# A transformer block on one core: the input projection on the unnormalised x, with w_ada's product moved to the output stage

## What is computed

```python
def rms_norm(x, g):
    y = x * rsqrt(mean(x * x, -1) + 1e-6) * g

h = rms_norm(x, norm_mix_pre)
proj = h @ w_in                      # 1024 x 2560: q, k, v and 14 tiles for the time mix
p = p + (p_prev - p) * rwkv_shift_mix          # p_prev: p moved by one token
scores = q @ k.T * scale + rel_bias[bucket(rel)]   # attention's bias table
...
x = x + rms_norm(mix @ w_out, norm_mix_post)   # the output stage
...
shift, scale, gate = split(silu(c) @ w_ada + b_ada, 3)   # used first behind the FFN
```

## Time and profile before

| what | us |
|---|---|
| runs: median of 3 (lowest, highest) | 3296.24 (3292.69, 3300.53) |
| profiled execution: span, first to last instruction | 3291.8 |
| TensorE matmul busy | 2815.3 (86%) |
| VectorE busy | 1213.9 (37%) |
| ScalarE busy | 726.0 (22%) |
| GpSimd busy | 795.9 (24%) |

### The profile page before, as it was taken

How to read it: one execution, slowest core, us unless ns; L and a number is a source line. 1 busy time by engine, 2 the same in 40 slices (tenths; PEclk the granted TensorE clock), 3 DMA queues, 4 the chain that set the end, 5 groups by cost and what they waited for, 6 DMA issues and landing times.

```text
span 3291.8 us, 45652 instructions
## 1 busy us (share of the span) xinstructions
PE 2815.3 (86%) x17970; PEld 2240.3 (68%) x17970; DVE 1213.9 (37%) x1572; ACT 726.0 (22%) x1050; POOL 795.9 (24%) x448
## 2 busy tenths in 40 slices
PE   2999766888889779999999999994999947879886
PEld 1787446878776558888888888882788836653375
DVE  2544554344443363213313313316100055544343
ACT  2101551111121222102102202102101253225521
POOL 1344000000001223433434343340333333210011
PEclk7999676687789889999999999996899955558988
DMA  5411000000001011111111111112111100000031
GB/s 162 154 39 57 0 18 15 2 3 3 2 28 71 32 71 51 51 45 51 45 51 45 51 49 47 51 45 115 75 59 51 39 26 1 0 3 1 0 122 58
DMA packets 34892, 146.85 MB, mean 45 GB/s; under 512 B 3656, under 2 KB 5832, under 8 KB 33608
## 3 DMA queue, kind: packets, MB, share of 16 engines
q1 hardware_dynamic: 23184, 84.42, 7.6%
q10 hardware_dynamic: 11576, 60.50, 5.0%
HBM read 124.46 MB, written 20.45 MB: 44 GB/s over the span
## 4 chain that ended last, share of the span: by engine, by line
PE 76%; DVE 14%; ACT 5%; issue 3%; DMA 2%; DVEq 1%; ACTq 0%; POOL 0%; POOLq 0%
PE ps L370 52%; PE ps L715 2%; PE ps L531 2%; ACT ab L76 1%; DVE s_m L76 1%; PE ps L768 1%; DVE x_lo L76 1%; DVE proj L76 1%; DVE xx L76 1%; PE ps L556 1%; DVE ps L76 1%; DMA bias_table<-bias_row 1%; PE ps L547 1%; PE ps L530 1%; DVE zz L76 1%
## 5 line engine op out<-in xcount | busy, mean ns | idle before, releaser
L302 POOL TENSOR_TENSOR w_hi<-w_raw,small 128x1024 fp32r<-128x1024 f32 x161 | 306.2, 1902 | 2256.6 <-PE ps L370 2249.8
L370 PE MATMUL ps<-x_hi,w_hi 128*128 128x512 f32 x2064 | 647.4, 395 | 85.1 <-DVE x_lo L76 78.7
L370 PE MATMUL ps<-x_lo,w_hi 128*128 128x512 f32 x2064 | 643.1, 393 | 0.0
L370 PE MATMUL ps<-x_hi,w_lo 128*128 128x512 f32 x2064 | 641.7, 392 | 0.0
L370 PEld LDWEIGHTS ps<-x_hi,w_hi 128*128 128x128 f32 x2064 | 388.7, 190 | 179.7 <-issue 72.4
L370 PEld LDWEIGHTS ps<-x_lo,w_hi 128*128 128x128 f32 x2064 | 392.4, 190 | 82.8
L370 PEld LDWEIGHTS ps<-x_hi,w_lo 128*128 128x128 f32 x2064 | 391.9, 190 | 82.7
L305 POOL TENSOR_TENSOR w_lo<-w_raw,w_hi 128x1024 fp32r<-128x1024 f32 x161 | 406.0, 2522 | 12.7
L76 DVE SCALAR_TENSOR_TENSOR cv<-ps,cst,cv 128x1023 f32<-128x1023 f32 x64 | 82.1, 1282 | 258.1 <-ACT cv L76 252.7
L370 PE MATMUL ps<-f_hi,w_lo 128*128 128x512 f32 x512 | 157.6, 389 | 0.0
L370 PE MATMUL ps<-f_hi,w_hi 128*128 128x512 f32 x512 | 157.6, 389 | 0.0
(11 more groups left out here) (255 smaller groups left out, 3917.4 us busy)
## 6 DMA issues: line engine op xcount, KB each, us to landing
w_raw<-wall SPq DMA_DIRECT2D x161, 512.0 KB, 3.4
ada_w<-wada ACTq DMA_DIRECT2D x24, 512.0 KB, 5.4
x_spill<-x ACTq DMA_DIRECT2D x2, 4096.0 KB, 11.0
x<-x_spill ACTq DMA_DIRECT2D x2, 4096.0 KB, 13.3
x_in<-xT ACTq DMA_DIRECT2D x2, 2048.0 KB, 12.0
x<-xT ACTq DMA_DIRECT2D x1, 4096.0 KB, 13.6
gate_spill<-gate_st ACTq DMA_DIRECT2D x8, 512.0 KB, 2.6
gate_in<-gate_spill ACTq DMA_DIRECT2D x8, 512.0 KB, 3.4
```

The costliest lines, as they stand in the source:

```text
L302: nc.gpsimd.tensor_tensor(w_hi[:, u, :, :], w_raw[:, u, :, :], sm["one"].unsqueeze(2).to_broadcast([P, KT, P]), ALU.mult).then_inc(S("w_hi ...
L370: last = mm(ps[:, 2 * u + h, :], w[:, u, k, :], x[:, k, h * 512:(h + 1) * 512], start=(k == 0 and w is w_hi and x is hi), stop=(k == KT - ...
```

## The change

The parameters that are needed first stand at the front of `cst` and are loaded by themselves; the rest follows behind x, which comes in eight loads of one tile. ScalarE makes x_hi straight from `x * g` as a tile lands, and its square after it; VectorE makes x_lo. TensorE takes gemm 0 one column at a time as x_lo comes, gemm 1 two columns behind it, with a norm sum after the even steps 2 to 8 of both; gemm 2 goes into banks 6 and 7. VectorE takes the reciprocal into `rs0` and evicts all twenty gemms itself, times `rs0` (`scaled`). The bias product comes behind gemm 3, its table is written and read while ScalarE has only one copy to make. w_ada's loads (a ring of four, three ahead of each y1 tile), the 24 steps of `modulation` (six ahead of each pair sum) and its products move to the output stage. Events that happen once share three semaphores (`once`); the lines that differ by that alone are left out below, as are the ones for `pairs_of`, `ada_w` and `ada_acc`, which get other places in SBUF.

```diff
@@ tensor
-            pe.wait_ge(S("cst_in"), 16)
-            pe.wait_ge(S("neg_row"), 1)
-            mm(ps[0:8, 0, 0:384], par("rel_bias", ...), par("onehot", ...))...(S("bias_mm"), 1)
-            norm_sum(0)
-            pe.wait_ge(S("bias_cp"), 1)
-            gemm(0, 0, x_hi, x_lo, first=True, parts=("x_lo_done", 0))
-            gemm(1, 1, x_hi, x_lo, first=True)
-            gemm(2, 0, x_hi, x_lo)
+            pe.wait_ge(S("par_in"), 16)
+            pe.wait_ge(S("w_split"), 1)
+            for step in range(KT + 2):
+                if step < KT:
+                    pe.wait_ge(S("x_lo_done"), step + 1)
+                    last = column(0, 0, step)
+                    if step == KT - 1:
+                        last.then_inc(S("gemm_mm"), 1)
+                if step == 2:
+                    pe.wait_ge(S("w_split"), 2)
+                if step >= 2:
+                    last = column(2, 1, step - 2)
+                    if step == KT + 1:
+                        last.then_inc(S("gemm_mm"), 1)
+                if step in (2, 4, 6, 8):
+                    norm_part(0, step // 2 - 1)
+            pe.wait_ge(S("w_split"), 3)
+            for k in range(KT):
+                last = column(6, 0, k)
+            last.then_inc(S("gemm_mm"), 1)
             gemm(3, 1, x_hi, x_lo)
+            pe.wait_ge(S("cst_in"), 16)
+            pe.wait_ge(*once("neg_row"))
+            pe.wait_ge(*once("rs0_done"))
+            mm(ps[0:8, 4, 0:384], par("rel_bias", ...), par("onehot", ...))...(once("bias_mm")[0], 1)
             gemm(4, 0, x_hi, x_lo)
             gemm(5, 1, x_hi, x_lo)
-            pe.wait_ge(S("one"), 1)
-            pe.wait_ge(S("ada_acc"), ADA_N)
-            for j in range(ADA_N):
-                last = mm(ps[:, 7, j:j + 1], ada_acc[...], sm["one"], start=True, stop=True)
-            last.then_inc(S("ada_mm"), 1)
+            gemm(6, 0, x_hi, x_lo)
             pe.wait_ge(S("gemm_evac"), 6)
-            turn(raw[:, 1, :], 4)
-            with pe.Fori(3, 10) as i:
+            turn(raw[:, 1, :], 6)
+            gemm(7, 1, x_hi, x_lo)
+            with pe.Fori(4, 10) as i:
...
             norm_sum(1)
+            pe.wait_ge(S("gemm_evac"), G_FFN)
+            pe.wait_ge(S("ada_acc"), ADA_N)
+            for j in range(ADA_N):
+                last = mm(ps[:, 0, j:j + 1], ada_acc[...], sm["one"], start=True, stop=True)
+            last.then_inc(once("ada_mm")[0], 1)
             norm_sum(2)
+            pe.wait_ge(*once("ada_done"))
@@ scalar
-            act.dma_start(x_in[:, 0:4, :], ...).then_inc(S("x_in0"), 16)
-            act.dma_start(x_in[:, 4:8, :], ...).then_inc(S("x_in1"), 16)
-            act.dma_start(cst[:, :], dr["cst"]).then_inc(S("cst_in"), 16)
+            act.dma_start(cst[:, 0:N_PAR], dr["cst"][:, 0:N_PAR]).then_inc(S("par_in"), 16)
+            for k in range(KT):
+                act.dma_start(x_in[:, k, :], dr["xT"][:, k * T:(k + 1) * T]).then_inc(S(f"x_in{k}"), 16)
+            act.dma_start(cst[:, N_PAR:], dr["cst"][:, N_PAR:]).then_inc(S("cst_in"), 16)
...
+            act.wait_ge(S("par_in"), 16)
+            for k in range(KT):
+                act.wait_ge(S(f"x_in{k}"), 16)
+                fn(x_hi[:, k, :], x_in[:, k, :], ACT.Identity, scale=par("g_mix_pre", k, 1))...
+                if k >= 2:
+                    act.wait_ge(S("norm_pair"), k // 2)
+                fn(sq_a[:, k % 2, :], x_in[:, k, :], ACT.Square).then_inc(S("norm_sq"), 1)
+            root(0)
+            act.wait_ge(*once("bias_mm"))
             copy(bias_row[0:8, :], ps[0:8, 4, 0:384])...
             act.dma_start(bias_dram, bias_row...).then_inc(S("bias_out"), 16)
+            act.wait_ge(S("turn_mm"), 1)
+            copy(proj[:, 5, :], pair(6)).then_inc(S("turn_cp"), 1)
             act.wait_ge(S("bias_out"), 16)
             act.dma_start(bias[:, :, :], ...).then_inc(S("bias_in"), 16)
-            high(0, lambda k: nrm_a[:, k % 2, :], "h_done")
-            for n in range(ADA_RING, 2 * ADA_RING):
-                ada_load(n)
-            for g in range(6):
-                for n in range(2 * ADA_RING + 3 * g, min(2 * ADA_RING + 3 * g + 3, ADA_N)):
-                    ada_load(n)
-                act.wait_ge(S("gemm_mm"), g + 1)
-                copy(proj[:, g, :] if g < 5 else raw[:, 1, :], pair(2 * (g % 2))).then_inc(S("gemm_evac"), 1)
...
+            act.wait_ge(S("cst_in"), 16)
+            fn(sm["silu_c"], par("c"), ACT.Silu).then_inc(once("c_silu")[0], 1)
             def y1_tile(k):
                 g = G_OUT + k
+                for n in range(3 * k, 3 * k + 3):
+                    ada_load(n)
                 act.wait_ge(S("gemm_mm"), g + 1)
                 copy(y1[:, k, :], pair(2 * (g % 2))).then_inc(S("gemm_evac"), 1)
@@ vector
-            for j in range(4):
-                norm_pair(0, j)
-            apply_all(0, 0, nrm_a, ...)
-            for n in range(ADA_N):
-                modulation(n)
-            dve.wait_ge(S("ada_mm"), 1)
-            tt(sm["ada"], ps[:, 7, 0:24], par("b_ada"), ALU.add)
-            ts(sm["ada"][:, 8:16], sm["ada"][:, 8:16], 1.0, None, ALU.add).then_inc(S("ada_done"), 1)
+            for k in range(KT):
+                dve.wait_ge(S("x_hi_done"), k + 1)
+                stt(x_lo[:, k, :], x_in[:, k, :], par("g_mix_pre", k, 1), x_hi[:, k, :].bitcast(F32),
+                    ALU.mult, ALU.subtract).then_inc(S("x_lo_done"), 1)
+                if k % 2:
+                    norm_pair(0, k // 2)
+            dve.wait_ge(S("norm_root"), 1)
+            reciprocal(rs0[:, :], rs_of(0)).then_inc(once("rs0_done")[0], 1)
+            def scaled(g, out, b):
+                dve.wait_ge(S("gemm_mm"), g + 1)
+                tt(out, pair(b), rs0[:, :], ALU.mult).then_inc(S("gemm_evac"), 1)
+            for g in range(5):
+                scaled(g, proj[:, g, :], 6 if g == 2 else 2 * (g % 2))
+            scaled(5, raw[:, 1, :], 2)
             def shift(g, j, s):
-                dve.wait_ge(S("gemm_evac"), g + 1)
+                scaled(g, raw[:, s, :], 2 * s)
                 tt(dif[:, s, 1:], raw[:, s, 0:T - 1], raw[:, s, 1:], ALU.subtract)
...
+            dve.wait_ge(*once("c_silu"))
             for j in range(4):
+                for n in range(6 * j, 6 * j + 6):
+                    modulation(n)
                 norm_pair(1, j)
...
             norm_pair(2, 3)
+            dve.wait_ge(*once("ada_mm"))
+            tt(sm["ada"], ps[:, 0, 0:24], par("b_ada"), ALU.add)
+            ts(sm["ada"][:, 8:16], sm["ada"][:, 8:16], 1.0, None, ALU.add).then_inc(once("ada_done")[0], 1)
             apply_all(2, 2, nrm_a, ...)
```

More of the change, by code:

```diff
@@ L95, in S, with once @@
             return sems[name]
+        def once(event):
+            sem = next(n for n, events in ONCE.items() if event in events)
+            return S(sem), ONCE[sem].index(event) + 1
         def at(name, shape, unit, dt=F32, off=0):
@@ L380, in turn, with norm_part @@
                 last.then_inc(S("turn_mm"), 1)
+            def norm_part(n, j):
+                pe.wait_ge(S("norm_pair"), 4 * n + j + 1)
+                for h in range(2):
+                    last = mm(rs_of(n)[:, h * 512:(h + 1) * 512], par("mean_all").to_broadcast([P, P]),
+                              pairs_of[n][:, j % 2, h * 512:(h + 1) * 512], start=(j == 0), stop=(j == 3),
+                              skip_group_check=True)
+                last.then_inc(S("norm_mm"), 1)
             def norm_sum(n):
@@ L384, in norm_sum, with column @@
                 for j in range(KT // 2):
-                    pe.wait_ge(S("norm_pair"), 4 * n + j + 1)
+                    norm_part(n, j)
+            def column(b, u, k):
+                for w, x in ((w_hi, x_hi), (w_hi, x_lo), (w_lo, x_hi)):
                     for h in range(2):
-                        last = mm(rs_of(n)[:, h * 512:(h + 1) * 512], par("mean_all").to_broadcast([P, P]),
-                                  pairs_of[n][:, j % 2, h * 512:(h + 1) * 512], start=(j == 0), stop=(j == 3),
+                        last = mm(ps[:, b + h, :], w[:, u, k, :], x[:, k, h * 512:(h + 1) * 512],
+                                  start=(k == 0 and w is w_hi and x is x_hi), stop=(k == KT - 1 and w is w_lo),
@@ L403, in _ @@
-            gemm(2, 0, x_hi, x_lo)
-            gemm(3, 1, x_hi, x_lo)
+                return last
+            pe.wait_ge(S("par_in"), 16)
[14 more added lines that the diff above has]
+                    norm_part(0, step // 2 - 1)
@@ L405, in _ @@
+            pe.wait_ge(S("w_split"), 3)
+            for k in range(KT):
+                last = column(6, 0, k)
+            last.then_inc(S("gemm_mm"), 1)
+            gemm(3, 1, x_hi, x_lo)
+            pe.wait_ge(S("cst_in"), 16)
+            pe.wait_ge(*once("neg_row"))
+            pe.wait_ge(*once("rs0_done"))
+            mm(ps[0:8, 4, 0:384], par("rel_bias", p1=N_BUCKETS + 1), par("onehot", p1=N_BUCKETS + 1),
+               start=True, stop=True).then_inc(once("bias_mm")[0], 1)
             gemm(4, 0, x_hi, x_lo)
```

(6 more changed lines are left out.)

90 lines of the change are left out of this document (40 added, 50 removed).

## The result

The changed kernel takes **3248.62 us** (median of 4 runs, 3247.14 to 3250.62), the kernel before 3294.47 us beside it (4 runs, 3289.98 to 3300.53): ratio 0.9865, interval 0.9851 to 0.9879. That is 45.9 us less, where the prediction had 62.4 less (3233.8) and a range that ended at 3247. The sign was right; the size was wrong, and the median lies 1.6 us outside the range.

A forecast was written before the change was run, and what follows sets the result against it. TensorE's chain bounds the first stage, so an earlier start shortens the end. First stage -70.1, evictions +0.2, output stage +7.5 give -62.4 us: span 3291.8 to 3229.4, median 3233.8, range 3220 to 3247.

The forecast's parts named there:

- the removed wait in attention: Attention: the wait that the change removes was already met long before, so its removal gives 0.
- the shared semaphores: Whole kernel: letting events that happen once share semaphores costs nothing.
- (c): Rival: bias table's write and weight loads hinder each other, three loads up to 5 us late, +15, 3249; chance 0.04.
- (b): Rival, output stage: loads behind x's 4 MB delay ScalarE's evictions, up to 30 us more, 3264; chance 0.07.
- The first stage: From the start to gemm 19's end: ends at 246.2 against 316.3, 70.1 us sooner.
- Start: First GEMM matmul: TensorE starts at 11.5 us, after split 0 and x_lo 0; bounds 10.2 to 12.8.
- Step 2: First stage: waits for split 1 and x_lo 2 until 19.6; TensorE idles 3.1 us, plus 1.1 of clock.
- Norm sums: First stage, steps 2 to 9: four sums of 2.0 us on TensorE's path, 8.0 more.
- Gemm 3: First stage: banks scaled out at 56.8, wanted at 58.7, margin 1.9 us; if missed, 0 to 3 late.
- Bias product and transposes: First stage on TensorE: bias product 0.8 us (between 0 and 2.0), transposes 1.8.
- Evictions: VectorE's evictions are covered under GEMMs; only after gemm 19 open, 1.22 for ScalarE's 1.03: +0.2 us.
- The output stage: Its end: late loads and modulations delay the last pair sum, +7.5 us (bounds +4 and +9); earlier all is slack.

The follow-up runs named there:

- a_mod8: Changed kernel with w_ada's loads four a tile over six output tiles and its products ahead of the first three pair sums: 3239.91 us.
- a_pad64: Changed kernel with 64 empty instructions at the head of TensorE's program: 3225.66 us, ratio 0.9799 to the kernel before.

## Why the prediction was wrong, point by point

**The step that failed** is one that the sum did not have. It went from gemm 19 to the output stage with two zeros ("the removed wait in attention was met long before: 0", "the shared semaphores cost nothing"), taking it that code which the change does not touch runs as before. It does not: the change puts 95 more instructions ahead of TensorE's recurrence loop, and the loop takes 24.0 us more, about 3.4 for each of seven jumps back; 95 empty instructions in the kernel before cost it 23.2 by themselves. The trace of the kernel before held the warning, TensorE's seven gaps of up to 3.9 us on "issue" in that loop, 26 us in all; the prediction reads no view of that stage. No rival named it either; (c) named 3249, nearly the measured time, and (b) up to 3264, but by ways that did not happen: that (c) comes so close is chance. The Trainium skill ("Runtime: NRT & Kernel Launch", section "Instruction fetch mechanics") says that code is fetched in blocks of 256 instructions ahead of use, and that a taken branch whose target is not at hand waits for its block; the gaps at each jump back agree, 3.7 us in the mean before and 4.9 after. With blocks of that size the runs can be put in the order of the head's place (an estimate from that figure: instructions past its place in the kernel before, whole blocks left out): 0, 31 and 63 took 457.9, 458.5 and 459.9 us, 95 took 481.9 and 481.1, 127 took 466.7, 159 took 462.2 and 458.6, 223 took 459.8. So the slow places begin between 63 and 95, and the cost has faded again by 159. That the wait depends on where the head lies the Trainium skill does not say; the runs do. Bounds for that term, an estimate from the rows of the kernel before, would have been, below, nothing, and above, another gap like those there at each jump: 26 us. With them the range would have held the result.

**The first stage** was right, 3.9 us too small: -74.0 for -70.1.
- *Start*: 12.3 for 11.5, within its bounds; but what ended last was x's first tile (7.7) with table load, x_hi and x_lo behind it, not split 0.
- *Step 2*: 18.18 for 19.6, after 1.04 us of idle in place of 3.1, and no 1.1 us of clock behind it: the granted clock is 1.00 from 16 to 44 us. The splits came sooner than in the earlier trace rows, likely since w_ada's loads no longer share the DMA engines with the weight tiles (not tested alone). The mechanism that made x_lo long was right (1.91 and 2.86 us beside splits).
- *Norm sums*: 1.72 us for 2.0. With the earlier step 2, gemm 1 ends at 44.6 for 47.8.
- *Gemm 3*: its banks were scaled out at 53.6, 1.9 us before it wanted them; no wait. That this is the very margin forecast is partly luck, since both times came 3.2 us earlier than forecast. Scaled evictions took 1.23 us.
- *Bias product and transposes*: 0.7 and 0.9 us for 0.8 and 1.8. So gemm 19 ends at 242.4 for 246.2.
- *Weight loads beside the table's write*: one landed late (the split at 90.65 waited 7.98 us for it), and TensorE did not; rival (c) fell.

**Evictions**: +0.2 forecast; from gemm 19's end to the first scores it was 3.3 us before and 2.8 after, so the +0.2 did not show.

**The output stage** was right in mechanism and 2.1 us too small: +9.6 for +7.5, just past its upper bound of +9. The modulation held by the split, the buffer's wait on ScalarE, the last loads and the two modulations behind them are all in the trace. The last load was issued 7.8 us behind the last GEMM and landed 5.4 later, the median of the earlier trace rows; the prediction's own chain gives +8.5 with that figure, and the pair sum ended 8.6 later. The other 1.0 is a term it did not have: the norm sum behind the longer idle ran at a mean granted clock of 0.54 for 0.73. The early part went as forecast too: the first modulation waited for the loads behind x's 4 MB, tile 1 was evicted late (1001.79, after 11.67 us of idle), and the output GEMMs took 87.3 us where they took 87.4 before (rival (b) fell). a_mod8 takes 8.7 us of it back.

**The sum again**: -74.0 first stage, -0.4 eviction, -0.2 up to the recurrence, +24.0 in it, +0.1 up to the last output GEMM, +9.5 tail, -2.1 behind it: -43.1 of span. The -2.1 is within what two profiles of the same code differ by. The forecast for the span, 3229.4, is thus missed by 19.3 us and the one for the median by 14.8: the prediction put the median 4.4 above the span, and here it lies at the span, which hid a part of the error by luck. Without the loop the terms would have come to -67, a little better than the -62.4 forecast; a_pad64, which is the changed kernel without most of the loop's loss, is at 3225.66, inside the range.

## What to carry to other kernels

Where an engine's gaps on "issue" stand at the jumps of a loop, an edit anywhere ahead of that loop in the engine's program can change its time. Here one loop showed it; the later ones, moved by 64 instructions, did not. Count the instructions that the edit adds there, give the term a bound of the gap times the turns, and try a few empty instructions before the edit is judged. And before a stage is put at zero, read its waits in the kernel before, most of all those that no engine caused.

When work is moved under a long GEMM stage, end it before the last tiles. Here the six products between the last two pair sums were on the path, however much slack the stage had before.

## What the runs showed of the hardware that was not expected

- The same loop of 1831 instructions a turn, with the same data, takes 458.5 to 481.9 us by its place in the program; the kernel before lost 0.85% by 95 empty instructions.
- The gaps cost more than their length: in the changed kernel 14.8 us of the 24 are idle time, and 9.2 are more busy time for the same matmuls, at a mean granted clock of 0.72 for 0.75.
- A large VectorE instruction that reads two SBUF tensors and began during a half of a split on GpSimd ended 1.08 to 1.09 us after that half, in all 87 such cases in the traces of the two kernels (among them the pair sum in the earlier trace rows, x_lo at 10.21 and 12.58, and the two large instructions of all 14 shifts in each kernel). Those with one operand in PSUM did not wait: the 1.22 us sum into `f_acc` of the earlier trace rows took 1.22 beside a split as well.
